# Expert gates of a PEER layer by one-hot matmuls: bf16 operands in three exact terms in place of float32

## What is computed

```python
def block(xt):                       # PEER, a block of tokens
    ...                              # two top-16 lists a head, then the best 16 of their sums
    experts = e1 * N_KEYS + e2       # 8 heads x 16 picks = 128 experts a token
    gate = jax.nn.softmax(sc, axis=-1)
    ue = u[experts]
    act = jax.nn.gelu(jnp.einsum('thkd,td->thk', ue, xt)) * gate
    return jnp.einsum('thk,thkd->td', act, v[experts])
```

## Time and profile before

| | before |
|---|---|
| median of 3 runs | 5477.85 us (5475.43 to 5478.51) |
| the profiled execution | 5480.13 us |
| its span in the profile | 5478.5 us |
| mean granted TensorE clock, share of 2.4 GHz | 0.962 |
| gate steps | 64, about 3090 to 4016 us |

### The profile page before, as it was taken

How to read it: one execution, slowest core, us unless ns; L and a number is a source line. 1 busy time by engine, 2 the same in 40 slices (tenths; PEclk the granted TensorE clock), 3 DMA queues, 4 the chain that set the end, 5 groups by cost and what they waited for, 6 DMA issues and landing times. The chain is left out here.

```text
span 5478.5 us, 70752 instructions
## 1 busy us (share of the span) xinstructions
PE 5095.6 (93%) x25566; PEld 4196.8 (77%) x25566; DVE 2874.3 (52%) x6216; ACT 1476.2 (27%) x2141; POOL 349.9 (6%) x420
## 2 busy tenths in 40 slices
PE   4599998999978699899999999999969999999998
PEld 1388886777667577788888888888858888888887
DVE  6511001777767543456666455555545555555556
ACT  1212121556634222322222222222221111111111
POOL 1100000000067210000000000000000000000000
PEclk7699899999989899999999999999989999999999
DMA  7322222333233452222222243333445555555554
GB/s 279 116 94 99 107 79 76 107 119 127 103 115 115 162 167 93 88 90 85 88 85 100 84 163 135 152 147 134 164 147 147 141 149 143 145 147 141 149 142 134
DMA packets 441187, 692.67 MB, mean 126 GB/s; under 512 B 284736, under 2 KB 300496, under 8 KB 435752
## 3 DMA queue, kind: packets, MB, share of 16 engines
q1 hardware_dynamic: 412488, 572.68, 31.8%
q0 software_dynamic: 25184, 105.18, 5.5%
q10 hardware_dynamic: 3328, 12.58, 0.6%
HBM read 470.02 MB, written 220.36 MB: 126 GB/s over the span
## 5 line engine op out<-in xcount | busy, mean ns | idle before, releaser
L1978 PE MATMUL ph_hid_ps<-ph_n_hi,ph_u_hi 128*128 128x512 f32 x2176 | 855.5, 393 | 7.8 <-DVE ph_u_lo L2111 7.8
L1978 PE MATMUL ph_hid_ps<-ph_n_lo,ph_u_hi 128*128 128x512 f32 x2176 | 848.6, 390 | 0.0
L1978 PE MATMUL ph_hid_ps<-ph_n_hi,ph_u_lo 128*128 128x512 f32 x2176 | 848.1, 390 | 0.0
L2363 PE MATMUL px_out_ps<-px_v_hi,px_weight_hi 128*128 128x512 f32 x2048 | 798.0, 390 | 49.0 <-DVEq L2414 49.0
L2363 PE MATMUL px_out_ps<-px_v_lo,px_weight_hi 128*128 128x512 f32 x2048 | 797.7, 389 | 0.0
L2363 PE MATMUL px_out_ps<-px_v_hi,px_weight_lo 128*128 128x512 f32 x2048 | 797.6, 389 | 0.0
L2442 DVE TENSOR_TENSOR held_tiles<-held_tiles,px_out_ps 128x512 f32<-128x512 f32 x512 | 350.2, 685 | 594.3 <-PE px_out_ps L2363 594.3
L2111 DVE TENSOR_TENSOR ph_u_lo<-ph_u_raw,ph_u_hi 128x1024 fp32r<-128x1024 f32 x136 | 166.6, 1225 | 693.1 <-ACT ph_u_hi L2032 692.7
L2363 PEld LDWEIGHTS px_out_ps<-px_v_hi,px_weight_hi 128*128 128x128 f32 x2048 | 385.2, 188 | 129.2 <-DVEq L2414 49.2
L1978 PEld LDWEIGHTS ph_hid_ps<-ph_n_hi,ph_u_hi 128*128 128x128 f32 x2176 | 409.9, 188 | 91.2 <-DVE ph_u_lo L2111 8.2
L1978 PEld LDWEIGHTS ph_hid_ps<-ph_n_hi,ph_u_lo 128*128 128x128 f32 x2176 | 409.5, 188 | 85.6
(11 more groups left out here) (306 smaller groups left out, 8047.2 us busy)
## 6 DMA issues: line engine op xcount, KB each, us to landing
ph_u_raw<-in_tiles SPq DMA_DIRECT2D x136, 512.0 KB, 3.5
scratch_hidden<-ph_hidden SPq DMA_DIRECT2D x128, 512.0 KB, 2.6
scratch_gate_tiles<-ph_gates SPq DMA_DIRECT2D x16, 4096.0 KB, 13.1
px_v_raw<-in_v_experts SPq DMA_DIRECT2D x128, 512.0 KB, 3.5
px_raw<-scratch_hidden SPq DMA_DIRECT2D x128, 512.0 KB, 5.3
px_gate<-scratch_gate_tiles SPq DMA_DIRECT2D x128, 512.0 KB, 6.5
mr_w<-in_ada_w POOLq DMA_DIRECT2D x6, 4096.0 KB, 20.1
mb_w_raw<-in_w_branch POOLq DMA_DIRECT2D x48, 512.0 KB, 3.9
```

What stands on the lines that cost most here:

```text
L1978: mm = pe.matmul(hid_ps[r][:, c * HALF:(c + 1) * HALF], u[r][a][:, k, :], n2[b][:, k, c * HALF:(c + 1) * HALF], start=(k == 0 and a + b == ...
L2363: mm = pe.matmul(out_ps[b][:], weight[q][j][wp][:, t * P:(t + 1) * P], v[q][j][vp][:, c * HALF:(c + 1) * HALF], start=(j == 0 and wp + vp ...
```

## The change

The gate products get bf16 operands. The row one-hot holds only 0 and 1 and is exact in bf16. The weight is split into three bf16 terms, each the rounding of what the terms before leave over, and the product is the sum of three matmuls in the same PSUM bank, all with the row one-hot as the stationary operand:

- At the stage's start DVE makes `share[0]` and `share[1]` (the first two bf16 terms of all weights) and leaves the remainder, in float32, in `chosenT[:, 2, :]`: two conversions and two subtractions of 128x1024, each waiting for the one before.
- In each bank DVE makes `row_hot` (bf16), the plain column one-hot `col_hot` (bf16, one comparison over 4 tokens, signals `col_ready[b]`), waits for its own `col_ready[b]`, and multiplies it with `share[0]` and with `share[1]` (4 tokens at a time, the share of a token repeated over 128 columns) into `term[0][b]` and `term[1][b]`.
- ACT makes `term[2][b]`: one copy a token of `col_hot`, with the remainder as its per-partition scale, 16 a step, ahead of `take_hidden`; it signals `third_ready[b]`.
- PE waits for `third_ready[b]` too, and does three bf16 matmuls a token in place of one in float32.
- `row_hot` halves in size, two `share` tiles come, `col_hot` and the terms lie in slabs 0, 1, 6 and 7 of `held`.

```diff
-        row_hot = [sp.sb(f"row_hot{b}", [P, TOK, NK]) for b in range(NBANK)]
+        row_hot = [sp.sb(f"row_hot{b}", [P, TOK, NK], BF16) for b in range(NBANK)]
+        share = [sp.sb(f"share{n}", [P, S], BF16) for n in range(2)]
...
-        col_hot = [held[:, b // 2, (b % 2) * HALF:(b % 2 + 1) * HALF].rearrange("p (t n) -> p t n", t=TOK) for b in range(NBANK)]
+
+        def in_held(slab, b):
+            return held[:, slab, :].bitcast(BF16)[:, b * HALF:(b + 1) * HALF].rearrange("p (t n) -> p t n", t=TOK)
+
+        col_hot = [in_held(0, b) for b in range(NBANK)]
+        term = [[in_held(slab, b) for b in range(NBANK)] for slab in (1, 6, 7)]
...
                         pe.wait_ge(hot_ready[b], j + 1)
                         pe.wait_ge(gates_taken[b], j + 1)
+                        pe.wait_ge(third_ready[b], j + 1)
                         for t in range(TOK):
-                            mm = pe.matmul(gate_ps[b][:, t, :], row_hot[b][:, t, :], col_hot[b][:, t, :], start=True, stop=True)
+                            for n in range(3):
+                                mm = pe.matmul(gate_ps[b][:, t, :], row_hot[b][:, t, :], term[n][b][:, t, :], start=(n == 0), stop=(n == 2))
                         mm.then_inc(gates_mm[b], 1)
...
                     r, m = x % 2, 36 + 4 * k + (4 * s + x) // 2
+                    for b in range(NBANK):
+                        act.wait_ge(col_ready[b], j + 1)
+                        for t in range(TOK):
+                            ins = act.activation(term[2][b][:, t, :], col_hot[b][:, t, :], ACT.Copy,
+                                                 scale=chosenT[:, 2, bass.ds(j * PER_STEP + (b * TOK + t), 1)])
+                        ins.then_inc(third_ready[b], 1)
                     take_hidden(r, m, m - 1 if r == 0 else m - 7)
...
                 dve.wait_ge(turned, 6)
+                own = Steps(dve, share_step)
+                for n in range(2):
+                    own.of(dve.tensor_copy(share[n][:], chosenT[:, 2, :]))
+                    own.wait()
+                    own.of(dve.tensor_tensor(chosenT[:, 2, :], chosenT[:, 2, :], share[n][:], ALU.subtract))
+                    own.wait()
...
-                        for t in range(TOK):
-                            tok = bass.ds(j * PER_STEP + (b * TOK + t), 1)
-                            ins = dve.tensor_scalar(col_hot[b][:, t, :], iota[:], chosenT[:, 1, tok], chosenT[:, 2, tok],
-                                                    ALU.is_equal, ALU.mult)
+                        toks = bass.ds(j * PER_STEP + b * TOK, TOK)
+                        dve.tensor_tensor(col_hot[b], iota[:].unsqueeze(1).to_broadcast([P, TOK, NK]),
+                                          chosenT[:, 1, toks].unsqueeze(2).to_broadcast([P, TOK, NK]), ALU.is_equal).then_inc(col_ready[b], 1)
+                        dve.wait_ge(col_ready[b], j + 1)
+                        for n in range(2):
+                            ins = dve.tensor_tensor(term[n][b], col_hot[b], share[n][:, toks].unsqueeze(2).to_broadcast([P, TOK, NK]), ALU.mult)
                         ins.then_inc(hot_ready[b], 1)
```

More of the change, by code:

```diff
@@ L1883, in stage_peer_topk @@
         turned = sp.sem("turned")
+        share_step = sp.sem("share_step")
+        col_ready = [sp.sem(f"col_ready{b}") for b in range(NBANK)]
         hot_ready = [sp.sem(f"hot_ready{b}") for b in range(NBANK)]
+        third_ready = [sp.sem(f"third_ready{b}") for b in range(NBANK)]
         gates_mm = [sp.sem(f"gates_mm{b}") for b in range(NBANK)]
```

## The result

The changed kernel takes 5428.18 us (median of 4 runs, 5424.24 to 5434.71) against 5476.64 (4 runs, 5474.76 to 5478.51) of the kernel before beside it: ratio 0.9913, 95% interval 0.9896 to 0.993. The profiled execution took 5434.71, with a span of 5433.0: 45.5 less than the span before.

The account below looks back on a forecast made before the run. PE's own stream was taken to bound the gate steps, 14.46 us each. Saving 0.36 a step gave -23.0 us, the stage's start +1.9, together -21.1: 5457 us, with an 8-in-10 range of 5440 to 5502.

Parts of the forecast that it names:

- the spacing of the gate matmuls: Gate part on PE: bf16 matmuls start 0.066 us apart, saving 0.36 us a step, -23.0 us over 64 steps.
- two independent rows: Support for 0.066 us: an attention-stage bf16 pair, and the tile's 0.013 us beyond streaming added to 0.053 for 128 columns.
- the case of 0.056: Faster than forecast: gate matmuls 0.056 us apart, a gain of 24 us, 5454 us; chance 0.06 including packed products.
- the ring: Loop through DVE and ACT from `low` to `low`, never passing PE: 13.75 us against PE's step of 14.10.
- its first rival: DVE and ACT's loop sets the step from 14.06 us; chance 0.13 for 5463 to 5480, 0.12 beyond.
- The rival with packed products: DVE's products packed and gate spacing 0.056 us: step 13.64, time 5427 us; within a shared chance of 0.06.
- The turn: Every 8 steps DVE stands 2.43 us at its first bank; this uses up cover, and PE still wins barely.
- The start: Stage start: DVE's conversions and subtractions take 4.0 us before the first bank, so PE waits once, +1.9 us.
- No clock effect: Rival on PE's gate parts: granted clock falls to 1.2 GHz, costing 3.2 us a step; chance 0.03.
- The weight loads: Rival on PE's gate parts: weight loads widen the spacing to 0.075 to 0.09 us, around 5500 us; chance 0.10.
- the rule against the change: Trainium skill's 81 ns a matmul in long streams: gate part 3.9 us, 20 us more, kernel about 5500.
- the lower bound: Gate matmul spacing at half the float32 one, 0.056 us, giving a gate part of 2.7 us.

## Why the prediction was wrong in size

**Step that failed: the spacing of the gate matmuls, a term of the sum.** "I take 0.066", from one bf16 pair. The term measured 0.056. The pair itself was read rightly, but it stands behind a float32 matmul, and the first pair behind one is 0.066 apart in the changed kernel too; the 46 other spacings are 0.056. The argument "two independent rows give it" did not hold either: the second row, the 0.013 beyond streaming, was of the tile's float32 matmuls of 512 columns. The gate part saves 0.822 where 0.36 was forecast (3.457 - 2.635, the handover the same, 0.34 from the last gate matmul's start to the tile's second in both). Over the whole step 0.793 is left, since from the tile's second matmul to the next gate part it is 10.70 for 10.66. The cause of these 0.03 to 0.04 was not looked for. (The 0.03 lie inside the tile, from its second to its last matmul: 10.467 for 10.437.) 63 x 0.793 = 50.0 for 23.0: these 27 us are as large as the whole miss, 48.5 measured for 21.1. That it comes out so closely is luck. The turns took 4.6 and the start 1.4 more than forecast; the last gate part gave 0.8, the earlier first gate part 1.95 and the rest of the span 0.7, and the medians lie 3.0 further apart than the two profiled spans.

**Why the right spacing wouldn't have been enough.** The prediction had the case of 0.056 and gave it 5454, "then the ring sets the step" at 14.055. That value was 13.75 and an eighth of DVE's 2.43 us at the turn. Both parts were too large. (The 14.06 from which its first rival lets the ring set the step doesn't follow from its own sum: with 2.44 us a turn in the ring, PE's 112.8 is reached at (112.8 - 2.44) / 8 = 13.80.) The ring by the rows above: 1.14 from `low` to the first bank, three banks 7.92, row 0.60, column 0.68, 0.14 until ACT starts, copies 1.18, `take_hidden` 0.90, `high` to `low` 1.08, which is 13.64, and 13.646 in the loop; it is the forecast's sum with four terms smaller by 0.02 to 0.04. And DVE's standstill is gone. No row of before could promise that, but the edit might have suggested it: a turn of DVE's program was getting shorter (342 recorded instructions, now 278) and ACT's longer (75, now 331). So the ring stayed 0.03 below PE's step. The rival with packed products had that step, 13.64, and its 5427 is where the time came out, without any packed product (0.688 each).

**The turn.** Forecast: a wait eating ring cover, no cost to PE. Measured: 4.9 to 7.9 us on ACT in three profiles of the kernel, and 3.3 to 6.7 lost in the stage. The place was right, the engine and the price wrong.

**The start.** +1.9 forecast, +3.3 measured. The row for 3100.82 was of an execution in which the tile ahead ran partly at a lower clock; with the tile ending 1.95 us earlier PE asks for the banks that much sooner, so the two figures aren't of the same start. What PE waits for are DVE's products, not the copies (without them 3.3 stay). That the two conversions and two subtractions cause most of it is confirmed by making them earlier (0.8 left).

**What was right.** PE's stream sets the ordinary step (shown by taking the copies away). A product with bf16 operands, one of them repeated, costs what the comparison costs: 0.688 for 0.682. The wait on DVE's own one-hot with a computed address: 0.14 idle and a bank of 2.64, for 0.16 and 2.65. Copies 0.39 long, 0.295 apart, for 0.40 and 0.305. The ring exists and closes at the copies (shown by one more copy). No clock effect: 1.00 in the stage.

**The rivals.** The ring does not take over, but it was nearer than the sum said, 0.03 against 0.35. The weight loads don't show: 0.056 in 47 spacings, whatever the stationary operand or bank. The 81 ns which the Trainium skill gives, TensorE: Matmul & The Clock Gate, section Back-to-back issue gap, for a long stream of weight load and matmul is not what these traces show; its isolated gap, 56, is. With what the runs show, the rule against the change deserved less than its 0.10, and the lower bound more.

## What to carry to other kernels

A spacing taken from one pair holds the handover into it; read the spacing of a stream from three or more alike instructions, and where the trace has none, give the lower bound a forecast of its own instead of a margin. When an edit moves computed addresses from one engine's loop to another's, the standstill at the loop's turn can move with them: ask who waits there, and look in the profile's DMA queues for loads of instructions. A ring below PE's step costs nothing until it is longer, and then everything: measure its slack by adding one instruction to it.

## What was not expected of the hardware

- A bf16 matmul of 128 columns with its own weight load starts 0.056 us after the one ahead, in groups of 16 and of 48, also with alternating operands and banks; 0.066 between the first two behind a float32 matmul. The float32 form of before needed 0.1115, so three bf16 products cost 0.168 where one float32 product in two passes cost 0.223.
- The idle time behind a jump back is 2.4 us on DVE before, 4.9 to 7.9 us on ACT in three profiles after (1.8 to 4.5 with one more copy), and none on ACT with 128 fewer instructions in a turn or without the loop. It ends 1.5 to 1.6 us after a load of instructions on ACT, 2.0 on DVE; with the shorter turn such loads are absent.
- Some 5.3 us of it on ACT cost the changed kernel nothing, since the 16 copies then run without waiting between banks (4.78 us in one go).
